# First four weight units opened together in four banks and taken by input block, in five pieces

## The chip, the cores and the metric

One core of one Trainium2 chip runs the program. The metric is the device time of one execution in microseconds (us). Engines: PE multiplies matrices, DVE and ACT work on vectors, POOL sets constants, SP issues transfers; ACT issues some too.

## What is computed

Two transformer blocks over 256 tokens of width 1024, in float32. The change touches only the beginning: the first norm and the first input projection.

```python
def first_block(x, mem, norm_mix, w_in, ...):
    h = h + hybrid_mixer(rmsnorm(h, norm_mix[i]), w_in[i], ...)
...
    proj = n @ w_in
    z, xBC, dt_raw, q, k, v, r, a1, g_ssd, g_gla = jnp.split(proj, idx, axis=-1)
```

## The kernel before

**Units.** All large weights come as a stream of 366 weight units `w[u]`, each 128 x 1024 floats (512 KB): 128 output columns, and 1024 inputs as eight blocks of 128 (`KB` = 8). A ring of four slots holds them (`raw`, `RING` = 4). Unit u goes into slot u % 4.

**Exact products.** Each operand is split into a high part and a low part of lower precision. ACT makes the high part of a unit (`split_hi`, L1163, `whi`), DVE the low part as a difference (`split_lo`, L1670, `wlo`). The input is split likewise, one block at a time: `xh` by ACT (L1209), `xl` by DVE (`operand_lo`, L1677). A unit is then three products for each of its eight blocks, high x high, high x low, low x high: 24 products of 256 columns, added up in one bank of `acc` (four banks, unit u in bank u % 4). DVE empties a bank by multiplying it with `rstd` (an eviction, L1828), the reciprocal root of the mean square that the norm needs. So units can be multiplied before the norm is known, but a bank can't be emptied before.

**Order.** Each engine has its own program, and semaphores tie them. SP issues units 0, the two halves of x, unit 1, the small weights `wsmall`, units 2 and 3; after that it issues a unit when `split_lo` has freed its slot (L380). ACT issues the parameters `par`.

- PE: 14 warm-up products (L713), unit 0 block by block as `xl` comes (L476 to L478), unit 1 (L717, L718, L721), `small_products` (L596 to L598), `stream_stats` (the mean squares, L559 and L563), then the loop over m = 2, 3, ...: `unit`, and after m = 3 the gates (L609).
- ACT: unit 0's high part, eight `xh`, unit 1's, eight squares of x (L1167) with the small weights between them, units 2 and 3, then `rms` (the root, L1181, L1183).
- DVE: unit 0's low part, eight `xl`, unit 1's low part, sums of the squares (L1763 to L1773), units 2 and 3, `inverse_rms` (L1710 to L1715: `rstd`, and `rstdh`, half of it), then the loop: eviction, taps of the convolution (L1795), low part of unit m + 4. At m = 0 it also reads the small products.

ACT's loop makes the high part of unit m + 4, then the first tap of the evicted bank; at m = 1 it loads a table and computes a softplus.

Of the kernel before, what the change touches and what calls it, by code (L numbers as in the profile page):

```python
# [23 lines left out]
P = 128  # L24
F32 = mybir.dt.float32
# [4 lines left out]
ALU = mybir.AluOpType  # L30
# [97 lines left out]
NPAR = _c  # L128
CHUNK_AT = {38: (0, 2), 40: (1, 3), 43: (4, 5)}
# [18 lines left out]
def blocks_kernel(nc, w, wsmall, wa2, par, xT, memT, metaT, out):  # L148
    with ExitStack() as ctx:
# [160 lines left out]
        def hidden(T):  # L310
# [12 lines left out]
        par_in, x_in, x2_in, meta_in, ws_in, wa_in, mem_in = [sem(n) for n in  # L323
            ("par_in", "x_in", "x2_in", "meta_in", "ws_in", "wa_in", "mem_in")]
# [41 lines left out]
        def _(sp_):  # L366
            sp_.dma_start(raw[:, 0, :], w[0, :, :]).then_inc(landed[0], 16)
            sp_.dma_start(hT[:, 0:4, META:T2], xT[:, 0:4, :]).then_inc(x_in, 16)
            sp_.dma_start(hT[:, 4:8, META:T2], xT[:, 4:8, :]).then_inc(x2_in, 16)
            sp_.dma_start(raw[:, 1, :], w[1, :, :]).then_inc(landed[1], 16)  # L370
            sp_.dma_start(wsr, wsmall).then_inc(ws_in, 16)
            for j in range(2, RING):
                sp_.dma_start(raw[:, j, :], w[j, :, :]).then_inc(landed[j], 16)
# [99 lines left out]
        def _(pe):  # L473
# [236 lines left out]

            pe.wait_ge(consts, 2)
            for n in range(14):
                nc.tensor.matmul(mix[:, 2, 0:P], mean1024[:, :], mean1024[:, :], start=True, stop=True)  # L713
            unit("xbc", 0, 0, xh1, xl1, T1, ready=(xl_ready, 0))
            pe.wait_ge(hi_ready, 2)
            for k in range(KB):
                nc.tensor.matmul(acc[:, 1, 0:T1], whi[:, 1, k, :], xh1[:, k, 0:T1], start=k == 0, stop=False)  # L717
                nc.tensor.matmul(acc[:, 1, 0:T1], whi[:, 1, k, :], xl1[:, k, 0:T1], start=False, stop=False)  # L718
            pe.wait_ge(lo_ready, 2)
            for k in range(KB):  # L720
                last = nc.tensor.matmul(acc[:, 1, 0:T1], wlo[:, 1, k, :], xh1[:, k, 0:T1], start=False, stop=k == KB - 1)  # L721
            last.then_inc(unit_done, 1)
            small_products()
            pe.wait_ge(consts, 15)
            stream_stats("mix", T1, tiles1)
            m = 0
            for phase, count in (("xbc", 12), ("q", 4), ("k", 4), ("v", 8), ("z", 8), ("r", 8), ("gs", 8), ("gg", 8)):
                for n in range(count):
# [3 lines left out]
                    elif m > 1:  # L732
                        unit(phase, n, n % 4, xh1, xl1, T1)
                    if m == 3:
                        gla_gates(0)
                        gla_gates(1)
# [419 lines left out]
        def _(act):  # L1156
            def split_hi(base, units=0):

                j = base % 4
                act.wait_ge(landed[j], units * 4 + 16 * (base // 4 + 1))  # L1160
                if base >= RING:
                    act.wait_ge(unit_done, units + (base - 3))
# [37 lines left out]
            act.dma_start(pr[:, :], par).then_inc(par_in, 16)  # L1200
            load_tables(3)
            split_hi(0)
            act.wait_ge(par_in, 16)
            for b in range(KB):
                if b == 4:
                    act.wait_ge(x2_in, 16)
                elif b == 0:
                    act.wait_ge(x_in, 16)
                act.activation(xh1[:, b, 0:T1], hT[:, b, META:T2], ACT.Copy, scale=g("mix", b)).then_inc(xh_ready, 1)  # L1209
            split_hi(1)  # L1210
            act.dma_start(wa[32:48, :], wa2).then_inc(wa_in, 16)
            for b in range(4):
                square(b, T1)
            act.wait_ge(ws_in, 16)
            act.activation(wsh[:, :, :].rearrange("p k c -> p (k c)"), wsr, ACT.Copy).then_inc(ws_ready, 1)
            for b in range(4, KB):
                square(b, T1)
            split_hi(2)
            split_hi(3)
# [445 lines left out]
        def _(dve):  # L1665
# [90 lines left out]
            dve.wait_ge(par_in, 16)  # L1756
            dve.tensor_scalar(halfc, pr[:, PC["convw"]:PC["convw"] + 60], 0.5, None, ALU.mult).then_inc(conv_step, 1)
            split_lo(0)
            for b in range(KB):
                operand_lo("mix", b, T1, b)  # L1760
            split_lo(1)
# [755 lines left out]
```

## Time and profile before

| | us |
|---|---|
| median of 3 runs | 1177.02 |
| lowest, highest | 1176.98, 1177.11 |
| span of the profiled execution | 1175.6 |
| PE busy in it | 1160.9 (99%) |
| DVE busy | 839.4 (71%) |
| ACT busy | 678.9 (58%) |

Times in the profile count from the start of the span. PE is busy nearly all the time; what it does at the beginning, and what it waits for there, is read from the list of waits and the timeline.

### The profile page before, as it was taken

To read this page: it belongs to the slowest core of one execution; us is meant where nothing else is said; L and a number is where in the kernel's file an instruction comes from. 1 tells how busy PE (TensorE), PEld (TensorE's weight loads), DVE (VectorE), ACT (ScalarE), POOL (GpSimd) and SP (SyncE) were. 2 spreads that over 40 slices of the span, in tenths; PEclk is the share of its full clock that TensorE was granted. 3 is DMA by queue.
4 is the path that set the end of the run, shared out by engine and by line. 5 is a ranking of instruction groups with operands and counts; after the bars stand their busy time and mean duration, and the time that the engine had idled before them with its cause. 6 is when DMAs were issued, how large, how long until landed. Compare 5 with 4: busy or idle time off the path is not lost.

```text
span 1175.6 us, 25261 instructions
## 1 busy us (share of the span) xinstructions
PE 1160.9 (99%) x9580; PEld 1140.0 (97%) x9580; DVE 839.4 (71%) x1249; ACT 678.9 (58%) x1029; POOL 46.6 (4%) x68
## 2 busy tenths in 40 slices
PE   8999999999999999999999999999999999999997
PEld 8999899999999999999999999999999999999997
DVE  7998767987856877776667748666545898776453
ACT  6755547656535666655556647656444777665442
POOL 2002311400000000000000000000000000000000
PEclk9999999999999999999999999999999999999998
DMA  6655434566553565656553426555565545666561
GB/s 226 190 174 175 128 107 143 183 225 187 164 159 126 164 201 190 191 185 189 180 152 113 123 73 209 176 171 190 190 180 170 160 144 165 212 182 193 182 194 54
DMA packets 56775, 197.51 MB, mean 168 GB/s; under 512 B 7153, under 2 KB 9457, under 8 KB 56577
## 3 DMA queue, kind: packets, MB, share of 16 engines
q1 hardware_dynamic: 54480, 193.68, 53.8%
q10 hardware_dynamic: 2224, 2.84, 0.8%
q8 instruction: 51, 0.84, 0.3%
q14 instruction: 20, 0.16, 0.0%
HBM read 195.45 MB, written 1.05 MB: 167 GB/s over the span
## 4 chain that ended last, share of the span: by engine, by line
PE 85%; DVE 9%; ACT 4%; issue 2%; DMA 0%; DVEq 0%; ACTq 0%
PE acc L482 14%; PE acc L483 14%; PE acc L488 14%; PE acc L476 11%; PE acc L478 11%; PE acc L477 11%; DVE wlo L1670 3%; ACT whi L1163 1%; PE acc L541 1%; PE acc L542 1%; PE acc L545 1%; PE mix L822 1%; PE mix L803 1%; DVE softp L2166 1%; DVE sp L2156 1%
## 5 line engine op out<-in xcount | busy, mean ns | idle before, releaser
L1670 DVE TENSOR_TENSOR wlo<-raw,whi 128x1024 fp32r<-128x1024 f32 x366 | 448.7, 1229 | 180.0 <-ACT whi L1163 179.8
L1163 ACT ACTIVATE whi<-raw 128x1024 fp32r<-128x1024 f32 x366 | 385.2, 1057 | 317.7 <-PE acc L488 158.5
L482 PE MATMUL acc<-xh,whi 128*128 128x256 f32 (+1 forms) x1448 | 358.2, 285 | 0.0
L483 PE MATMUL acc<-xl,whi 128*128 128x256 f32 (+1 forms) x1448 | 353.7, 282 | 0.0
L482 PEld LDWEIGHTS acc<-xh,whi 128*128 128x128 f32 x1448 | 271.8, 188 | 2.9 <-issue 2.3
L483 PEld LDWEIGHTS acc<-xl,whi 128*128 128x128 f32 x1448 | 272.7, 188 | 0.3
L488 PE MATMUL acc<-xh,wlo 128*128 128x256 f32 (+1 forms) x1448 | 202.2, 282 | 0.0
L478 PE MATMUL acc<-hh,wlo 128*128 128x256 f32 (+1 forms) x688 | 194.4, 283 | 0.0
L476 PE MATMUL acc<-hh,whi 128*128 128x256 f32 (+1 forms) x688 | 194.3, 282 | 0.0
L477 PE MATMUL acc<-hl,whi 128*128 128x256 f32 (+1 forms) x688 | 194.1, 282 | 0.0
L488 PEld LDWEIGHTS acc<-xh,wlo 128*128 128x128 f32 x1448 | 185.2, 188 | 0.0
L477 PEld LDWEIGHTS acc<-hl,whi 128*128 128x128 f32 x688 | 129.4, 188 | 0.0
L478 PEld LDWEIGHTS acc<-hh,wlo 128*128 128x128 f32 x688 | 129.3, 188 | 0.0
L476 PEld LDWEIGHTS acc<-hh,whi 128*128 128x128 f32 x688 | 129.3, 188 | 0.0
L476 PE MATMUL acc<-xh,whi 128*128 128x256 f32 (+1 forms) x272 | 77.3, 284 | 3.3 <-DVE xl L1677 3.3
L478 PE MATMUL acc<-xh,wlo 128*128 128x256 f32 (+1 forms) x272 | 76.6, 282 | 0.0
L477 PE MATMUL acc<-xl,whi 128*128 128x256 f32 (+1 forms) x272 | 76.6, 281 | 0.0
L476 PEld LDWEIGHTS acc<-xh,whi 128*128 128x128 f32 x272 | 51.1, 188 | 3.9 <-DVE wlo L1670 2.4
L482 PE MATMUL acc<-yh,whi 128*128 128x256 f32 (+1 forms) x224 | 54.3, 281 | 0.0
L483 PE MATMUL acc<-yl,whi 128*128 128x256 f32 (+1 forms) x224 | 54.3, 280 | 0.0
L477 PEld LDWEIGHTS acc<-xl,whi 128*128 128x128 f32 x272 | 51.2, 188 | 0.0
L478 PEld LDWEIGHTS acc<-xh,wlo 128*128 128x128 f32 x272 | 51.1, 188 | 0.0
(397 smaller groups left out, 1572.1 us busy)
## 6 DMA issues: line engine op xcount, KB each, us to landing
raw<-w SPq DMA_DIRECT2D x366, 512.0 KB, 3.7
hT<-xT SPq DMA_DIRECT2D x2, 512.0 KB, 6.3
mem<-memT ACTq DMA_DIRECT2D x1, 1024.0 KB, 7.3
rgw<-w ACTq DMA_DIRECT2D x2, 512.0 KB, 4.9
out<-hT SPq DMA_DIRECT2D x4, 128.0 KB, 2.5
out<-hT ACTq DMA_DIRECT2D x4, 128.0 KB, 2.8
xdt<-wsmall SPq DMA_DIRECT2D x1, 192.0 KB, 7.0
pr<-par ACTq DMA_DIRECT2D x1, 114.0 KB, 4.4
```

Source lines behind the costliest of these rows:

```text
L476: nc.tensor.matmul(dst, whi[:, slot, n, :], rh, start=first, stop=False)
L477: nc.tensor.matmul(dst, whi[:, slot, n, :], rl, start=False, stop=False)
L478: return nc.tensor.matmul(dst, wlo[:, slot, n, :], rh, start=False, stop=last)
L482: nc.tensor.matmul(dst, whi[:, slot, n, :], rh, start=first, stop=False)
L483: nc.tensor.matmul(dst, whi[:, slot, n, :], rl, start=False, stop=False)
L488: ins = nc.tensor.matmul(dst, wlo[:, slot, k, :], rh(k), start=False, stop=last and k == KB - 1)
L541: nc.tensor.matmul(dst, ah[:, k, at:at + n], whi[:, s:s + 2, k, :], start=k == 0, stop=False)
L542: nc.tensor.matmul(dst, al[:, k, at:at + n], whi[:, s:s + 2, k, :], start=False, stop=False)
L545: last = nc.tensor.matmul(dst, ah[:, k, at:at + n], wlo[:, s:s + 2, k, :], start=False, stop=k == KB - 1)
L803: last = nc.tensor.matmul(mix[:, h % 2, 256 * t:256 * t + 256], xqT[:, 2 * h + i, P * t:P * t + P], xkT[:, 2 * h + i, :], start=i == 0, st ...
L1163: act.activation(whi[:, j, :, :].rearrange("p k c -> p (k c)"), raw[:, j, :], ACT.Copy)\
L1670: dve.tensor_tensor(wlo[:, j, :, :].rearrange("p k c -> p (k c)"), raw[:, j, :], whi[:, j, :, :].rearrange("p k c -> p (k c)").bitcast(F32 ...
```

## The change

Units 0 to 3 are multiplied together, block by block, each into its own bank. Their weights and x come in five pieces by input block (`PIECES`): one block, one block, and three times two. A piece of weights is one transfer that takes the same blocks of all four units: 512 B (pieces 0, 1) or 1 KB (pieces 2 to 4) out of each 4 KB row. The first two pieces of x are issued by ACT, ahead of its table load, with only the eight columns of `par` that `xh` needs; the rest of `par` goes last on SP's queue. ACT splits a piece of x, then a piece of weights for all four units in one instruction; DVE follows with the low parts. PE takes a block in three groups of four products (high x high, high x low, low x high over the four units), and the last piece unit by unit. Then come the statistics, then the small products, then unit 4. The warm-up has 11 products. The slots of the ring are all freed by the last low part. The gates come after unit 4 and the small products are read by DVE at m = 1.

```diff
+PIECES = ((0, 1), (1, 2), (2, 4), (4, 6), (6, 8))
...
-            sp_.dma_start(raw[:, 0, :], w[0, :, :]).then_inc(landed[0], 16)
-            sp_.dma_start(hT[:, 0:4, META:T2], xT[:, 0:4, :]).then_inc(x_in, 16)
-            sp_.dma_start(hT[:, 4:8, META:T2], xT[:, 4:8, :]).then_inc(x2_in, 16)
-            sp_.dma_start(raw[:, 1, :], w[1, :, :]).then_inc(landed[1], 16)
+            for n, (a, b) in enumerate(PIECES):
+
+                if n >= 2:
+                    sp_.dma_start(hT[:, a:b, META:T2], xT[:, a:b, :]).then_inc(x_in[n], 16)
+                sp_.dma_start(raw[:, :, P * a:P * b], w[0:RING, :, P * a:P * b].rearrange("j p c -> p j c"))\
+                    .then_inc(w_in[n], 16)
             sp_.dma_start(wsr, wsmall).then_inc(ws_in, 16)
-            for j in range(2, RING):
-                sp_.dma_start(raw[:, j, :], w[j, :, :]).then_inc(landed[j], 16)
+            sp_.dma_start(pr[:, KB:NPAR], par[:, KB:NPAR]).then_inc(par_in, 16)
...
+            def open_block(k, n):
+
+
+                pe.wait_ge(xh_ready, k + 1)
+                pe.wait_ge(open_hi, n + 1)
+                for j in range(RING):
+                    nc.tensor.matmul(acc[:, j, 0:T1], whi[:, j, k, :], xh1[:, k, 0:T1], start=k == 0, stop=False)
+                pe.wait_ge(xl_ready, k + 1)
+                for j in range(RING):
+                    nc.tensor.matmul(acc[:, j, 0:T1], whi[:, j, k, :], xl1[:, k, 0:T1], start=False, stop=False)
+                pe.wait_ge(open_lo, n + 1)
+                for j in range(RING):
+                    nc.tensor.matmul(acc[:, j, 0:T1], wlo[:, j, k, :], xh1[:, k, 0:T1], start=False, stop=False)
+
             pe.wait_ge(consts, 2)
-            for n in range(14):
+            for n in range(11):
                 nc.tensor.matmul(mix[:, 2, 0:P], mean1024[:, :], mean1024[:, :], start=True, stop=True)
-            unit("xbc", 0, 0, xh1, xl1, T1, ready=(xl_ready, 0))
-            pe.wait_ge(hi_ready, 2)
-            for k in range(KB):
-                nc.tensor.matmul(acc[:, 1, 0:T1], whi[:, 1, k, :], xh1[:, k, 0:T1], start=k == 0, stop=False)
-                nc.tensor.matmul(acc[:, 1, 0:T1], whi[:, 1, k, :], xl1[:, k, 0:T1], start=False, stop=False)
-            pe.wait_ge(lo_ready, 2)
-            for k in range(KB):
-                last = nc.tensor.matmul(acc[:, 1, 0:T1], wlo[:, 1, k, :], xh1[:, k, 0:T1], start=False, stop=k == KB - 1)
-            last.then_inc(unit_done, 1)
-            small_products()
+            for n, (a, b) in enumerate(PIECES[:-1]):
+                for k in range(a, b):
+                    open_block(k, n)
+            pe.wait_ge(hi_ready, RING)
+            pe.wait_ge(xl_ready, KB)
+            for j in range(RING):
+                for k in range(*PIECES[-1]):
+                    high_products(acc[:, j, 0:T1], j, k, xh1[:, k, 0:T1], xl1[:, k, 0:T1], False)
+                if j == 0:
+                    pe.wait_ge(lo_ready, RING)
+                low_products(acc[:, j, 0:T1], j, range(*PIECES[-1]), lambda k: xh1[:, k, 0:T1], True)\
+                    .then_inc(unit_done, 1)
             pe.wait_ge(consts, 15)
             stream_stats("mix", T1, tiles1)
+            small_products()
             m = 0
             for phase, count in (("xbc", 12), ("q", 4), ("k", 4), ("v", 8), ("z", 8), ("r", 8), ("gs", 8), ("gg", 8)):
                 for n in range(count):
                     if phase == "v":
                         if n % 2:
                             token_pair(phase, n - 1, xh1, xl1, tiles1)
-                    elif m > 1:
+                    elif m >= RING:
...
-                    if m == 3:
+                    if m == 4:
...
-            act.dma_start(pr[:, :], par).then_inc(par_in, 16)
+            act.dma_start(pr[:, 0:KB], par[:, 0:KB]).then_inc(mixw_in, 16)
+            for n in range(2):
+                act.dma_start(hT[:, n, META:T2], xT[:, n, :]).then_inc(x_in[n], 16)
             load_tables(3)
-            split_hi(0)
-            act.wait_ge(par_in, 16)
-            for b in range(KB):
-                if b == 4:
-                    act.wait_ge(x2_in, 16)
-                elif b == 0:
-                    act.wait_ge(x_in, 16)
-                act.activation(xh1[:, b, 0:T1], hT[:, b, META:T2], ACT.Copy, scale=g("mix", b)).then_inc(xh_ready, 1)
-            split_hi(1)
+            act.wait_ge(mixw_in, 16)
+            for n, (a, b) in enumerate(PIECES):
+                act.wait_ge(x_in[n], 16)
+                for k in range(a, b):
+                    act.activation(xh1[:, k, 0:T1], hT[:, k, META:T2], ACT.Copy, scale=g("mix", k)).then_inc(xh_ready, 1)
+                act.wait_ge(w_in[n], 16)
+                act.activation(whi[:, :, a:b, :].rearrange("p j k c -> p j (k c)"), raw[:, :, P * a:P * b], ACT.Copy)\
+                    .then_inc(*((hi_ready, RING) if b == KB else (open_hi, 1)))
+                if n:
+                    for k in range(a if n > 1 else 0, b):
+                        square(k, T1)
             act.dma_start(wa[32:48, :], wa2).then_inc(wa_in, 16)
-            for b in range(4):
-                square(b, T1)
             act.wait_ge(ws_in, 16)
             act.activation(wsh[:, :, :].rearrange("p k c -> p (k c)"), wsr, ACT.Copy).then_inc(ws_ready, 1)
-            for b in range(4, KB):
-                square(b, T1)
-            split_hi(2)
-            split_hi(3)
+            act.wait_ge(par_in, 16)
             rms("mix", T1, (P, P))
...
-            dve.wait_ge(par_in, 16)
-            dve.tensor_scalar(halfc, pr[:, PC["convw"]:PC["convw"] + 60], 0.5, None, ALU.mult).then_inc(conv_step, 1)
-            split_lo(0)
-            for b in range(KB):
-                operand_lo("mix", b, T1, b)
-            split_lo(1)
-            dve.wait_ge(sq_ready, 4)
-            dve.tensor_tensor(sq[:, 2:4, 0:T1], sq[:, 0:2, 0:T1], sq[:, 2:4, 0:T1], ALU.add).then_inc(sum_ready, 1)
-            dve.wait_ge(ws_ready, 1)
-            dve.tensor_tensor(wsl[:, :, :].rearrange("p k c -> p (k c)"), wsr,
-                              wsh[:, :, :].rearrange("p k c -> p (k c)").bitcast(F32), ALU.subtract)\
-                .then_inc(wsl_ready, 1)
+            dve.wait_ge(mixw_in, 16)
+            for n, (a, b) in enumerate(PIECES):
+                for k in range(a, b):
+                    operand_lo("mix", k, T1, k)
+                dve.wait_ge(*((hi_ready, RING) if b == KB else (open_hi, n + 1)))
+                dve.tensor_tensor(wlo[:, :, a:b, :].rearrange("p j k c -> p j (k c)"), raw[:, :, P * a:P * b],
+                                  whi[:, :, a:b, :].rearrange("p j k c -> p j (k c)").bitcast(F32), ALU.subtract)\
+                    .then_inc(*((lo_ready, RING) if b == KB else (open_lo, 1)))
+                if b == 4:
+                    dve.wait_ge(sq_ready, 4)
+                    dve.tensor_tensor(sq[:, 2:4, 0:T1], sq[:, 0:2, 0:T1], sq[:, 2:4, 0:T1], ALU.add).then_inc(sum_ready, 1)
             dve.wait_ge(sq_ready, KB)
             dve.tensor_tensor(sq[:, 6:8, 0:T1], sq[:, 4:6, 0:T1], sq[:, 6:8, 0:T1], ALU.add).then_inc(sum_ready, 1)
             dve.wait_ge(sum_ready, 2)
             dve.tensor_tensor(sq[:, 6:8, 0:T1], sq[:, 2:4, 0:T1], sq[:, 6:8, 0:T1], ALU.add).then_inc(sum_ready, 1)
             dve.wait_ge(sum_ready, 3)
             dve.tensor_tensor(sq[:, 7, 0:T1], sq[:, 6, 0:T1], sq[:, 7, 0:T1], ALU.add).then_inc(sum_ready, 1)
-            split_lo(2)
-            split_lo(3)
+            dve.wait_ge(ws_ready, 1)
+            dve.tensor_tensor(wsl[:, :, :].rearrange("p k c -> p (k c)"), wsr,
+                              wsh[:, :, :].rearrange("p k c -> p (k c)").bitcast(F32), ALU.subtract)\
+                .then_inc(wsl_ready, 1)
+            dve.wait_ge(par_in, 16)
+            dve.tensor_scalar(halfc, pr[:, PC["convw"]:PC["convw"] + 60], 0.5, None, ALU.mult).then_inc(conv_step, 1)
             inverse_rms("mix", T1, (P, P), halved=True)
...
-                    if m == 0:
+                    if m == 1:
```

## Rows read from the trace of the kernel before

**Rows 1.** The page, busy time of the engines.
```profile
PE 1160.9 (99%) x9580; PEld 1140.0 (97%) x9580; DVE 839.4 (71%) x1249; ACT 678.9 (58%) x1029; POOL 46.6 (4%) x68
```
**Rows 2.** Waits of PE, 0 to 60 us: total, times, longest.
```profile
PE acc L476 <- DVE xl L1677: 2.2, 1, 2.2
```
**Rows 3.** Timeline of PE: start us, us, engine line op tile, count.
```profile
1.20 4.85 PE L713 MATMUL mix<-mean 128*128 128x128 f32 x28 [1.20 <-POOL mean L404]
8.30 0.36 PE L476 MATMUL acc<-xh,whi 128*128 128x256 f32 x1 [2.24 <-DVE xl L1677]
...
11.47 0.34 PE L717 MATMUL acc<-xh,whi 128*128 128x256 f32 x1
...
14.34 0.28 PE L596 MATMUL mix<-xh,wsh 128*48 128x256 f32 x1
...
17.14 0.60 PE L559 MATMUL mix<-sq,mean 128*128 128x256 f32 x2
...
17.94 0.36 PE L482 MATMUL acc<-xh,whi 128*128 128x256 f32 x1
...
23.71 1.99 PE L609 MATMUL mix<-xdt,bcn 16*128 16x256 f32 x8
25.63 0.38 PE L482 MATMUL acc<-xh,whi 128*128 128x256 f32 x1
```
**Rows 4.** Timelines of ACT and of DVE, the same columns.
```profile
5.08 1.06 ACT L1163 ACTIVATE whi<-raw 128x1024 fp32r<-128x1024 f32 x1 [2.53 <-DMA raw<-w]
7.12 2.90 ACT L1209 ACTIVATE xh<-hT,pr 128x256 fp32r<-128x256 f32 x7 [0.99 <-DMA hT<-xT]
...
11.28 1.32 ACT L1167 ACTIVATE sq<-hT 128x256 f32<-128x256 f32 x4
...
14.15 1.99 ACT L1163 ACTIVATE whi<-raw 128x1024 fp32r<-128x1024 f32 x2
...
7.66 3.29 DVE L1677 SCALAR_TENSOR_TENSOR xl<-hT,pr,xh 128x256 fp32r<-128x256 f32 x8
11.41 1.23 DVE L1670 TENSOR_TENSOR wlo<-raw,whi 128x1024 fp32r<-128x1024 f32 x1 [0.46 <-ACT whi L1163]
...
14.28 0.69 DVE L1769 TENSOR_TENSOR sq<-sq 128x512 f32<-128x512 f32 x1 [0.48 <-ACT sq L1167]
...
15.73 0.43 DVE L1773 TENSOR_TENSOR sq<-sq 128x256 f32<-128x256 f32 x1
...
20.57 0.29 DVE L1715 TENSOR_SCALAR rstdh<-rstd 128x256 f32<-128x256 f32 x1
...
21.62 0.41 DVE L1828 TENSOR_TENSOR convin<-acc,rstd 128x256 f32<-128x256 f32 x1
```
**Rows 5.** Transfers: count, KB, us from issue to landing; issues 0.81, 1.26, 1.73, 2.27, all.
```profile
raw<-w SPq DMA_DIRECT2D x1, 512.0 KB, 4.2
hT<-xT SPq DMA_DIRECT2D x1, 512.0 KB, 5.8
hT<-xT SPq DMA_DIRECT2D x1, 512.0 KB, 6.8
raw<-w SPq DMA_DIRECT2D x1, 512.0 KB, 7.6
raw<-w SPq DMA_DIRECT2D x366, 512.0 KB, 3.7
```
**Rows 6.** Windows: us, busy PE, PEld, DVE, ACT, POOL; clock, DMA share, GB/s.
```profile
2.00:3.00 1.00, 1.00 (x7) 1.00 (x6) 0.00 (x0) 0.55 (x1) 1.00 (x3) 1.00 0.99 144
...
7.00:8.00 1.00, 0.00 (x0) 0.00 (x0) 1.00 (x2) 0.88 (x3) 1.00 (x2) 1.00 1.12 423
```
**Rows 7.** Packets moved in 5.0 to 5.5, 6.5 to 7.0, 10.0 to 10.5 us.
```profile
DMA packets 133, 0.14 MB, mean 272 GB/s; under 512 B 0, under 2 KB 133, under 8 KB 133
DMA packets 192, 0.19 MB, mean 389 GB/s; under 512 B 5, under 2 KB 191, under 8 KB 192
DMA packets 56, 0.20 MB, mean 401 GB/s; under 512 B 7, under 2 KB 7, under 8 KB 56
```

More of the change, by code:

```diff
@@ L322, in blocks_kernel @@
         consts = sem("consts")
-        par_in, x_in, x2_in, meta_in, ws_in, wa_in, mem_in = [sem(n) for n in
-            ("par_in", "x_in", "x2_in", "meta_in", "ws_in", "wa_in", "mem_in")]
+        par_in, mixw_in, meta_in, ws_in, wa_in, mem_in = [sem(n) for n in
+            ("par_in", "mixw_in", "meta_in", "ws_in", "wa_in", "mem_in")]
+        x_in = [sem(f"x_in{n}") for n in range(len(PIECES))]
+        w_in = [sem(f"w_in{n}") for n in range(len(PIECES))]
+        open_hi, open_lo = sem("open_hi"), sem("open_lo")
         xh_ready, xl_ready, sq_ready = sem("xh_ready"), sem("xl_ready"), sem("sq_ready")
@@ L1159, in split_hi @@
                 j = base % 4
-                act.wait_ge(landed[j], units * 4 + 16 * (base // 4 + 1))
-                if base >= RING:
-                    act.wait_ge(unit_done, units + (base - 3))
+                act.wait_ge(landed[j], units * 4 + 16 * (base // 4))
+                act.wait_ge(unit_done, units + (base - 3))
                 act.activation(whi[:, j, :, :].rearrange("p k c -> p (k c)"), raw[:, j, :], ACT.Copy)\
```

## The prediction

> **What bounds the kernel now.** I read the page's busy table first: TensorE (PE) is busy 1160.9 of 1175.6 us [rows 1]. So the kernel is a PE stream that starts late, and only two things can shorten it: an earlier start, or fewer holes. The list of PE's waits up to 60 us names one wait for data, 2.2 us ahead of the first real product [rows 2]. The PE timeline shows the rest [rows 3]: warm-up from 1.20 to 6.05, a hole, first product at 8.30, then unit 0 (to 11.47), unit 1 (to 14.34), the 24 small products (14.34 to 17.14, so 2.80 us, 0.1167 us each), the statistics (to 17.94), units 2 and 3 (to 23.71, 2.88 us each) and the gates. From 8.30 on there is no hole; unit 0 takes 3.17 instead of 2.80 us, because xl is made one block each 0.41 us [rows 4].
>
> Why 8.30: weight unit 0 lands at 5.06 (issued 0.81, 4.2 us to landing; ACT starts its high part at 5.08), the first half of x at 7.06 (issued 1.26, 5.8 us) [rows 4, 5]. So the hole is a wait for x, which stands behind a whole unit of weights in the queue.
>
> **Yardstick.** At 23.71 PE has done units 0 to 3, the small products and the statistics. The changed kernel does the same work and goes on with unit 4 (the gates, 1.92 us, come one unit later, which is neutral). If its opening (the four units) ends at T, the gain is 23.71 less the time at which unit 4 can begin. All later stages are the same PE stream and shift with it.
>
> **From T to unit 4.** Statistics now come first, then the small products: 0.80 + 2.80, so PE is free at T + 3.6. But unit 4 needs bank 0 emptied, and that needs rstd. Before, the statistics began at 17.14, DVE's halved rstd (the step after rstd) ended at 20.86, and an eviction takes 0.41 [rows 3, 4]. So from the start of the statistics bank 0 is free after 3.72 + 0.41 + about 0.1 for the semaphore, 4.25 us, and PE waits some 0.65 us ahead of unit 4: a new hole. It was covered before, since units 2 and 3 went into empty banks while rstd was made. Hence **gain = 23.71 - 4.25 - T = 19.46 - T.**
>
> **What the opening needs.** 96 products at 0.1167 are 11.2 us. Let H(n) be the time at which ACT has finished the high part of piece n. The first eight products of a block take 0.93 us, then its low part must be there. DVE's low part of 1024 columns takes 1.23 [rows 4], so after a piece that PE stood waiting for, it waits about 0.35 us more. Pieces 2, 3 and 4 hold two blocks each (2.8 us of PE). So T is the largest of:
> - S + 11.2, S being the first product. By the rate below piece 0 lands near 4.7; its 512 columns take ACT 0.6 (a little over half of the 1.06 for 1024 [rows 4]). So S is 5.3 and this is 16.5;
> - H(2) + 0.35 + 8.4 + 0.1 for the semaphores, H(2) + 8.9;
> - H(3) + 6.1;
> - H(4) + 3.65 (here PE has only 4 products to do before it waits for the low part, so that wait is 0.85).
>
> The early start is therefore worth nothing by itself: if piece 2 comes late, PE does blocks 0 and 1 (2.8 us) and stands.
>
> **When the pieces come.** ACT's own work between piece 1's landing and H(2) is 0.6 for piece 1, two squares (1.32 for 4, so 0.66), two xh (2.90 for 7, so 0.82) and 1.0 for piece 2 (1.99 for two units), 3.1 us in all [rows 4]. So H(2) is the later of (piece 1 landed + 3.1) and (piece 2 landed + 1.05). The bytes: 0.39 MB a piece (w 0.262, x 0.131) for 0 and 1, and 0.787 for 2, 3 and 4; in sum 0.79 MB by piece 1, 1.57 by piece 2, 3.15 by piece 4. Little flows before 3.0 us (144 GB/s in the third microsecond); I count 0.15 MB [rows 6]. A transfer is reported landed some 0.9 us after the queue has moved all bytes up to its end: adding up the seven microseconds from 1 to 8 (the second and the last stand in rows 6), 0.641 MB (unit 0 and par) were through at 4.3 and reported at 5.06, and 1.69 MB (with all of x) at 7.4 and reported at 8.5 [rows 5, 6].
>
> The unknown is the rate r for this mixture. Weights now come in packets of 512 B (pieces 0, 1) and 1 KB. No row has 512 B. With 4 KB rows the queue moves 401 GB/s; pure 1 KB packets (x) go at 272 GB/s in one half microsecond and at 389 in another [rows 7]. The bounds are 200 GB/s (512 B packets a little quicker each than the slow 1 KB ones) and 400 (no loss). I take 320, a little under the middle of the two 1 KB rows, since five sixths of the bytes are in 1 KB packets.
>
> By r = 320: piece 1 lands at 3.0 + 0.64/0.32 + 0.9 = 5.9, piece 2 at 8.35, piece 3 at 10.8, piece 4 at 13.25. H(2) is the later of 9.0 and 9.4. T is the largest of 16.5, 9.4 + 8.9 = 18.3, 11.85 + 6.1 = 17.95 and 14.3 + 3.65 = 17.95. So T = 18.3 and the gain is **1.16 us**. By r = 400, H(2) is 8.6 (ACT's chain now binds), T = 17.5, gain 1.96. By r = 272, T = 19.6 (piece 4 binds), a loss of 0.15.
>
> A rule speaks against the change here. The Trainium skill, DMA: Bandwidth & Descriptors, "Why small descriptors are slow (HBM only)", says that each packet costs about three bus cycles beside its 32-byte beats; from that I estimate 512 B packets at 0.86 and 1 KB packets at 0.94 of the rate of 4 KB ones. By that rule r would be near 370 and the gain about 1.7 us; the 389 row agrees with it, the 272 row doesn't.
>
> **What costs nothing, and its cover.** Three warm-up products fewer (14 took 4.85 us, so 1.04 less [rows 3]) end the warm-up at 5.0, before S. The granted clock stayed at 1.00, the 2.4 GHz level, through the old hole of 2.2 us [rows 6], so a hole of this size costs only itself. The sums of the squares on DVE (14.28 to 16.16 before [rows 4]) follow the last low part and end near H(4) + 3.2, before T. wsmall and the rest of par now go last on SP's queue, behind 3.1 MB; they land near 14 and are wanted after T. Weight units 4 to 7 are issued only after the last low part (H(4) + 1.3, near 15.6) and all at once; a unit lands 3.7 us after its issue [rows 5], so unit 4 is there near 19.5 and its high part, behind ACT's root, near 21, against PE's 22.5. That cover is 1.5 us. Behind the eviction, DVE's work per unit (eviction 0.41, low part 1.23, taps) and ACT's table load and softplus are the same, but PE now stands 3.6 us closer to them. Adding their rows up, the high part of unit 6 comes about 1 us before PE wants it and the tightest eviction (unit 5's) 0.5 us. So I put no wait there.
>
> **Rivals.**
> - *Pieces come as quickly as 4 KB rows, and ACT's chain is shorter than I add.* T is 16.5 to 17.4, the time 1174.1 to 1175.0. For it: the 389 row. Against: ACT's 3.1 us cannot start before piece 1 is there, whose 0.79 MB is more than the 0.641 that landed at 5.06. Chance 0.12.
> - *Arrival becomes the bound (slower).* If runs of 512 B and 1 KB picked out of four units at once move at 200 to 250 GB/s, H(4) decides: at 250, piece 4 lands at 15.9, T = 20.6, 1178.2; at 200, T = 23.6, 1181.2. The break-even is r = 275; a loss of 0.2% is passed at r = 227. For it: the 272 row, and that every read now takes an eighth or a quarter of a 4 KB row. Against: 389 GB/s a microsecond later. Chance 0.13. The skill's DMA: Bandwidth & Descriptors, "Rules for kernel authors", asks to coalesce small transfers because mostly overhead is paid; here unit 1, queued behind x, was reported 1.4 us after it [rows 5], so no fixed cost is paid in series.
> - *The closeness costs.* DVE's low parts or ACT's table load come after PE wants them, in units 5 to 9, for 1 to 2 us in sum: 1176.9 to 1177.9. For it: margins of 0.5 to 1 us only. Against: DVE needs about 2.4 us a unit there, PE 2.8. Chance 0.10.
> - *Forecast*, r between 272 and 400: 1175.0 to 1177.2. Chance 0.65.
>
> **The numbers.** The profiled execution spans 1175.6 us; the median is 1177.02, so 1.4 us lie outside it and don't change. 1177.02 - 1.16 = 1175.9. Two tenths of a per cent, about what a measurement of this kernel can tell from no change, are 2.35 us, so faster means under 1174.67: most of the first rival, 0.09. Slower means over 1179.37: the second rival's slow end, 0.08. The range 1174.7 to 1178.4 leaves about 0.1 out on either side.
>
> **What would show it.** First product at 5 to 5.5; PE standing near 8 for about a microsecond, released by the high part of piece 2; opening over near 18.3; 0.65 us of idle time ahead of unit 4, released by the eviction; no hole afterwards. Wrong if the wait sits at piece 3 or 4 (r below 272), if there is none at all, or if holes show between units 5 and 9.

## The result: slower by a quarter of a per cent

| | before | after |
|---|---|---|
| median, us | 1177.44 (10 runs) | 1180.69 (10 runs) |
| span of the profiled execution, us | 1175.6 | 1178.2 |
| ratio after / before | | 1.0024 [1.0015, 1.0033] |

A gain of 1.16 us was forecast and a range of 1174.7 to 1178.4; the changed kernel is about 3 us slower and lies outside it. The ten runs of before that stand beside it have a median 0.4 us above that of the first three. One of the ten runs of the changed kernel took 4042.79 us, for a reason that nothing here shows, and the ratio is that of the other nine. Between the two profiled executions the change lost 2.6 us, and the traces show where.

PE first: the busy times, and all waits of PE up to 200 us (total, times, longest), in the profile of after. The lines are those of the changed kernel, 5 to 23 higher than before.

```profile
PE 1162.8 (99%) x9574; PEld 1140.5 (97%) x9574; DVE 839.3 (71%) x1250; ACT 679.1 (58%) x1030; POOL 46.2 (4%) x68
```
```profile
PE mix L732 <- POOL mean L409: 1.2, 1, 1.2
PE acc L722 <- ACT whi L1231: 1.1, 2, 0.9
PE mix L651 <- DVE bcn L1845: 1.0, 2, 0.5
PE acc L487 <- DVE convin L1851: 0.6, 1, 0.6
PE mix L636 <- DVE xdt L1942: 0.6, 1, 0.6
PE acc L546 <- ACT vt L1326: 0.4, 1, 0.4
PE mix L628 <- DVE xc L1916: 0.2, 1, 0.2
```

From 60 to 200 us the list of before has one line:

```profile
PE mix L646 <- DVE bcn L1822: 1.0, 2, 0.5
```

The 2.2 us wait for xl [rows 2] is gone, and the wait for bcn is as long as it was. The waits for whi and for convin, 1.7 us together, are of the kind that the forecast has. The last three are not: they are new, and they lie at 82 to 93 us, still within the first projection, at m = 23 to 25 of the loop, where the values' units are multiplied. PE's timeline in after, at the places that matter (start, time in the group, line, tile, count, idle time before):

```profile
8.45 0.71 PE L722 MATMUL acc<-xh,whi 128*128 128x256 f32 x4 [0.16 <-ACT whi L1231]
...
10.99 0.71 PE L722 MATMUL acc<-xh,whi 128*128 128x256 f32 x4 [0.91 <-ACT whi L1231]
...
19.81 0.59 PE L564 MATMUL mix<-sq,mean 128*128 128x256 f32 x2
24.19 0.36 PE L487 MATMUL acc<-xh,whi 128*128 128x256 f32 x1 [0.61 <-DVE convin L1851]
...
29.11 0.38 PE L487 MATMUL acc<-xh,whi 128*128 128x256 f32 x1
...
83.54 0.67 PE L628 MATMUL mix<-xc 128*128 128x256 f32 x2 [0.15 <-DVE xc L1916]
...
86.35 0.36 PE L546 MATMUL acc<-whi,xh 128*128 128x256 f32 x1 [0.40 <-ACT vt L1326]
...
93.30 0.66 PE L636 MATMUL mix<-ident,xc 128*128 128x128 f32 x4 [0.59 <-DVE xdt L1942]
93.72 0.42 PE L651 MATMUL mix<-cs,sel 128*128 128x384 f32 x1
```

The same work in the timeline of before:

```profile
28.54 0.28 PE L482 MATMUL acc<-xh,whi 128*128 128x256 f32 x1
...
82.45 0.59 PE L623 MATMUL mix<-xc 128*128 128x256 f32 x2
...
84.55 0.36 PE L541 MATMUL acc<-whi,xh 128*128 128x256 f32 x1
...
91.11 0.42 PE L646 MATMUL mix<-cs,sel 128*128 128x384 f32 x1
```

The opening is over (T) at 19.81, and unit 4 starts at 24.19 where before had reached that point at 23.71 [rows 3]. So PE leaves the opening only about half a microsecond late (0.57 us at unit 5, 28.54 against 29.11). Three holes later it is 1.09 us late at 83.54, 1.80 at 86.35 and **2.61 at 93.72**. (The starts are what counts here: the idle times listed add up to less, since the ends of products are modelled.) That is the whole loss; from there to the end it stays at 2.4 to 2.6.

DVE tells why. Its idle times between 20 and 90 us in before:

```profile
27.86 1.22 DVE L1670 TENSOR_TENSOR wlo<-raw,whi 128x1024 fp32r<-128x1024 f32 x1 [1.32 <-ACT whi L1163]
42.39 1.22 DVE L1670 TENSOR_TENSOR wlo<-raw,whi 128x1024 fp32r<-128x1024 f32 x1 [0.31 <-ACT whi L1163]
54.91 1.23 DVE L1670 TENSOR_TENSOR wlo<-raw,whi 128x1024 fp32r<-128x1024 f32 x1 [0.61 <-ACT whi L1163]
84.93 1.23 DVE L1670 TENSOR_TENSOR wlo<-raw,whi 128x1024 fp32r<-128x1024 f32 x1 [1.96 <-ACT whi L1163]
```

and in after, with the three instructions that follow the statistics ahead of them:

```profile
21.52 1.74 DVE L1731 RECIPROCAL rstd<-rt 128x256 f32<-128x256 f32 x1
23.29 0.29 DVE L1735 TENSOR_SCALAR rstdh<-rstd 128x256 f32<-128x256 f32 x1
23.62 0.42 DVE L1851 TENSOR_TENSOR convin<-acc,rstd 128x256 f32<-128x256 f32 x1
...
30.55 1.23 DVE L1690 TENSOR_TENSOR wlo<-raw,whi 128x1024 fp32r<-128x1024 f32 x1 [1.29 <-ACT whi L1184]
45.08 1.23 DVE L1690 TENSOR_TENSOR wlo<-raw,whi 128x1024 fp32r<-128x1024 f32 x1 [0.32 <-ACT whi L1184]
57.61 1.23 DVE L1690 TENSOR_TENSOR wlo<-raw,whi 128x1024 fp32r<-128x1024 f32 x1 [0.61 <-ACT whi L1184]
87.62 1.23 DVE L1690 TENSOR_TENSOR wlo<-raw,whi 128x1024 fp32r<-128x1024 f32 x1 [1.96 <-ACT whi L1184]
```

The same four waits have the same length, each 2.69 or 2.70 us later. From rstdh (20.57 in [rows 4], 23.29 here, 2.72 later) to 87.6 us DVE's program is moved as one rigid piece and makes nothing up: it is busy nearly all the time, and its few waits, for ACT's next high part, are as long as before, so ACT moves with it. The busy time of the engines in stretches of 10 us shows it in before already (PE, PEld, DVE, ACT, POOL, then clock, DMA share, GB/s):

```profile
30.00:40.00 10.00, 10.00 (x88) 9.87 (x87) 9.89 (x21) 5.06 (x8) 0.00 (x0) 1.00 0.53 160
...
60.00:70.00 10.00, 10.00 (x88) 10.00 (x87) 10.00 (x20) 5.90 (x9) 0.00 (x0) 1.00 0.69 197
70.00:80.00 10.00, 10.00 (x87) 10.00 (x86) 9.87 (x15) 3.29 (x4) 0.00 (x0) 1.00 0.57 168
```

DVE has 71% of the whole span [rows 1] but 94 to 100% of each 10 us from 30 to 80.

### The profile page after: what moved, and what is told of

Its sections match the earlier page's. It is cut to its first block, busy times and chain, and to the rows that moved or that the text cites. A ratio compares the mean times of both kernels' runs of the same rounds, so it can differ in the third digit from the quotient of the medians.

```text
span 1178.2 us, 25266 instructions
## 1 busy us (share of the span) xinstructions
PE 1162.8 (99%) x9574; PEld 1140.5 (97%) x9574; DVE 839.3 (71%) x1250; ACT 679.1 (58%) x1030; POOL 46.2 (4%) x68
## 4 chain that ended last, share of the span: by engine, by line
PE 86%; DVE 8%; ACT 4%; issue 1%; DMA 1%; SPq 0%; DVEq 0%; ACTq 0%
PE acc L487 15%; PE acc L488 15%; PE acc L493 15%; PE acc L481 11%; PE acc L483 10%; PE acc L482 10%; DVE wlo L1690 3%; ACT whi L1184 1%; PE acc L547 1%; PE acc L550 1%; PE acc L546 1%; DMA raw<-w 1%; PE mix L844 1%; PE mix L825 1%; DVE softp L2189 1%
## 5 line engine op out<-in xcount | busy, mean ns | idle before, releaser
L1690 DVE TENSOR_TENSOR wlo<-raw,whi 128x1024 fp32r<-128x1024 f32 x362 | 443.7, 1228 | 177.5 <-ACT whi L1184 177.3
L1184 ACT ACTIVATE whi<-raw 128x1024 fp32r<-128x1024 f32 x362 | 381.1, 1057 | 308.2 <-PE acc L493 153.7
L487 PE MATMUL acc<-xh,whi 128*128 128x256 f32 (+1 forms) x1440 | 356.4, 285 | 0.6 <-DVE convin L1851 0.6
L493 PEld LDWEIGHTS acc<-xh,wlo 128*128 128x128 f32 x1440 | 184.2, 188 | 0.0
L481 PE MATMUL acc<-xh,whi 128*128 128x256 f32 (+1 forms) x264 | 74.7, 283 | 1.1 <-DVE xl L1697 1.1
L483 PEld LDWEIGHTS acc<-xh,wlo 128*128 128x128 f32 x264 | 49.6, 188 | 0.0
```

Of the source, the lines that this page charges most:

```text
L481: nc.tensor.matmul(dst, whi[:, slot, n, :], rh, start=first, stop=False)
L483: return nc.tensor.matmul(dst, wlo[:, slot, n, :], rh, start=False, stop=last)
L487: nc.tensor.matmul(dst, whi[:, slot, n, :], rh, start=first, stop=False)
L493: ins = nc.tensor.matmul(dst, wlo[:, slot, k, :], rh(k), start=False, stop=last and k == KB - 1)
L1184: act.activation(whi[:, j, :, :].rearrange("p k c -> p (k c)"), raw[:, j, :], ACT.Copy)\
L1690: dve.tensor_tensor(wlo[:, j, :, :].rearrange("p k c -> p (k c)"), raw[:, j, :], whi[:, j, :, :].rearrange("p k c -> p (k c)").bitcast(F32 ...
```

## Experiments

**Theory D:** from rstd to some 92 us DVE (with ACT behind it) has no slack, and at 82 to 93 us PE has to wait for its results. So the end moves with the start of the statistics, whatever PE does in between. **Theory P**, the one of the prediction: PE's stream sets the end, so it moves with PE's own delay after the opening. Two quantities are compared in each kernel: the start of the statistics less 17.14 [rows 3], and the start of PE's first product of cs and sel less 91.11. PE's own delay is read at its first product of unit 5, against 28.54. Unless a number of executions is given, times in us come from the one profiled execution of each kernel, and ratios from all its runs.

**Statistics late, nothing else.** The kernel before, with the statistics after unit 2:

```diff
-            stream_stats("mix", T1, tiles1)
...
+                    if m == 2:
+                        stream_stats("mix", T1, tiles1)
```

> The kernel before, with only one thing moved: PE does the statistics (0.8 us) after unit 2 instead of ahead of it. PE's work and the transfers at the beginning are those of before. Theory D (DVE's program has no slack from the making of rstd up to about 90 us, so the kernel shifts with the start of the statistics): the statistics move from 17.14 to about 20.0, DVE's first eviction by 2.9 us, and PE stands for it between 80 and 95 us; the time is 2.4 to 2.9 us longer than before. Theory P (PE's stream sets the time from the first product on, as the prediction had it): only a hole of some 0.5 us ahead of the gates, which now wait for the small products to be read; 0.5 to 0.8 us longer than before.

Measured: 1.0027 [1.0015, 1.004]. The statistics start at 19.93 (+2.79), and cs and sel at 93.81 (+2.70): D's number. But it isn't a clean proof: in the profiled execution PE met a hole of 0.47 us and the gates, then the granted clock fell to the 1.2 GHz level for some 3.4 us, so PE itself was 2.06 us late at unit 5.

**DVE with less to do.** One of the taps of the convolution on 16 columns, in after and in before:

```diff
+                n = 16 if tap == 2 else T1
-                ... in0=convin[:, c, tap:tap + T1], ... in1=xc[:, c, :],
+                ... in0=convin[:, c, tap:tap + n], ... in1=xc[:, c, 0:n],
```

> The changed kernel, with DVE's load in the first 60 us cut: tap 2 of the convolution covers 16 of its 256 columns (so most of that tap is left out), about 0.25 us less for each of 12 instructions, 3 us in sum. Theory D: DVE catches up by unit 18, the waits of PE at 82 to 93 us go, and only the 0.6 us that PE itself has lost by unit 5 stays: 1.5 to 2.2 us less than the changed kernel. Rival A (the waits at 82 to 93 us come from ACT, whose exponentials stand ahead of the evictions of the values): no change, within 0.5 us of the changed kernel.

> The control of the run with the light tap: the kernel before with the same cut (tap 2 on 16 of 256 columns, most of it left out). Its PE waits for DVE only 1.0 us in this part of the program. Theory D: 0.3 to 1.1 us less than before, so less than the changed kernel gains from the same cut. If the cut takes 2 us or more off this kernel too, DVE is the bound in both and the cut says nothing on the change.

Measured: after goes to 1.0005 [0.9995, 1.0014], before to 0.9998 [0.9988, 1.0008]. The same relief is worth 0.2% in after and nothing in before. The 0.3 to 1.1 us expected of before didn't come: the 1.0 us that its PE waits for DVE (bcn) lies at 144 and 153 us and stays. PE's waits in the lightened after:

```profile
PE acc L722 <- ACT whi L1231: 3.0, 3, 1.6
PE mix L651 <- DVE bcn L1846: 1.0, 2, 0.5
PE acc L487 <- DVE convin L1852: 0.6, 1, 0.6
```

The three waits at 82 to 93 us are gone. The opening of this execution came late (whi 3.0 instead of 1.1 us, statistics +4.02), PE was 1.92 us behind at unit 5, and cs and sel stand at +2.12: this is theory P's behaviour, once DVE has slack.

**An earlier x.** All x on SP's queue, each piece ahead of its weights:

```diff
+                sp_.dma_start(hT[:, a:b, META:T2], xT[:, a:b, :]).then_inc(x_in[n], 16)
...
-            for n in range(2):
-                act.dma_start(hT[:, n, META:T2], xT[:, n, :]).then_inc(x_in[n], 16)
```

> The changed kernel, with the first two pieces of x issued on SP's queue, each ahead of its weights, in place of ACT's queue, where the second one took 5.4 us to land (7.25) while the weights of the same piece had landed at 5.15. If the two queues' sharing delayed piece 1 and through it ACT: piece 1 complete near 6.0, H(2) near 9.9 instead of 10.85, the opening over near 19.2 instead of 19.81 (piece 4 binds then), and by theory D as by theory P 0.5 to 0.7 us less than the changed kernel. If the queue's rate alone sets piece 2: H(2) within 0.3 us of 10.85 and no change.

Measured: 1.0043 [1.0026, 1.0059]. A miss: the first product came earlier (5.22), the pieces behind it later. The weights of piece 1 were taken up at 7.07 and those of piece 2 at 10.69, so PE waited 0.97 and 2.39 us. Statistics +3.49, cs and sel +3.43, although PE was only 1.36 late at unit 5.

**Statistics a unit earlier.** After, with the statistics ahead of the last products of unit 3:

```diff
+                if j == 2:
+                    pe.wait_ge(consts, 15)
+                    stream_stats("mix", T1, tiles1)
```

> The changed kernel, with the statistics one unit's products earlier: after unit 2's last products instead of unit 3's. Theory D (DVE's chain from rstd on has no slack): they start near 19.1 instead of 19.81 (the sums end at 18.7), everything after 91 us stands where the statistics' shift puts it, about 0.7 us less than the changed kernel. The hole of 0.6 us ahead of unit 4 closes too, because 0.7 us of products now lie behind the statistics, but by theory D that alone is worth nothing: if the hole closes and the shift after 91 us is the statistics' shift less 0.1, D holds; if the time falls by 1.2 us or more, the hole and the chain add up, and D is wrong.

Measured: 1.0021 [1.0011, 1.0031]. The 0.61 us ahead of unit 4 is gone, but the opening again came late in the profiled execution (whi 3.1 us): statistics +3.59, PE 1.47 late at unit 5, cs and sel +3.53. So the 0.7 us of time weren't gained, but the sign of theory D is there: the hole closes, and the later work stands where the statistics put it, less 0.06. An early start of the statistics helps only if the opening allows it.

**DVE's work moved, none left out.** ACT evicts the gates instead of DVE, and the halved rstd is made at m = 26, off the way to the first eviction. This, on the last kernel and on before:

```diff
-            inverse_rms("mix", T1, (P, P), halved=True)
+            inverse_rms("mix", T1, (P, P))
...
+                    if m == 26:
+                        dve.tensor_scalar(rstdh[:, 0:T1], rstd[:, 0:T1], 0.5, None, ALU.mult).then_inc(rstdh_ready, 1)
...
-                            ins = dve.tensor_scalar(gx[:, i, :], mix[:, BANK[f"gate{i // 2}"], ...
+                            ins = act.activation(fl(khk)[:, 256 * i:256 * i + 256], mix[:, BANK[f"gate{i // 2}"], ...
```

> The kernel with the early statistics, and 1.9 us of DVE's work between rstd and 91 us taken off that chain: ACT instead of DVE evicts the four gate tiles (1.64 us), and rstdh (0.3 us) is made at unit 26 instead of right behind rstd. Theory D: DVE's shift of 2.0 us is nearly used up by 80 us, PE's waits at 82 to 93 us mostly go, and what remains is PE's own shift at unit 5, near 0 with the early statistics: 2 to 2.6 us less than the changed kernel, within 0.8 us of the kernel before. Rival A (ACT is what is late at 82 to 93 us): ACT has 2 us more to do, and the time is that of the early statistics or longer.

> The control: the kernel before with the same 1.9 us of DVE's work moved. Theory D: PE waits only 1.0 us for DVE here, so 0 to 0.9 us less than before. If it gains as much as the changed kernel does, the move is worth something by itself and doesn't tell of the change.

Measured: 1.0000 [0.9991, 1.001] and 1.0003 [0.9993, 1.0013]. Again the move is worth 0.2% where the statistics are late, and nothing in before. In the first of the two, statistics +3.40, PE +1.19 at unit 5, cs and sel +1.53, and no wait is left at 82 to 93 us. ACT got the work that DVE lost, so with a late ACT as the cause (rival A) this kernel would have been no faster; that cause is ruled out.

**Fewer, larger pieces.** After with four pieces of two blocks, all x on SP's queue; then the same with early statistics; then with both and DVE's work moved:

```diff
-PIECES = ((0, 1), (1, 2), (2, 4), (4, 6), (6, 8))
+PIECES = ((0, 2), (2, 4), (4, 6), (6, 8))
```

> The changed kernel with four pieces of two blocks (no packets of 512 B for the weights, and fewer transfers) and all of x on SP's queue ahead of its weights. Up to the end of the second piece the same 1.57 MB are moved as by the run with x on SP, in 1536 packets instead of 2048. If the number of packets or transfers sets the arrival, the second piece lands about a microsecond earlier than there (10.7 us); if the bytes set it, at the same time. First product near 7.3 us. The opening ends between 18.9 and 20.6; by theory D the time is that of the kernel before plus the statistics' start less 17.14: 1.7 to 3.5 us longer than before.

> Pieces of two blocks with all of x on SP's queue, and the statistics one unit's products earlier. Theory D gives the shift against the kernel before, from 91 us on, as the start of the statistics less 17.14 and 0.08: they should start near 18.65, so a shift of 1.4 us, 1.0 to 1.8 us longer than before, though PE itself stands no later at unit 5 than before (about 0.5 us earlier). Theory P (PE's stream sets the time) gives 0.5 us less than before.

> The same with the 1.9 us of DVE's work taken off the chain behind rstd (gates evicted by ACT, rstdh made at unit 26). Theory D: DVE's shift of 1.4 us is used up, PE's own shift stays, about 0.5 us less than before; 1.5 to 2.3 us less than the run with the early statistics alone. If the early start were worth its 1 us of PE time once DVE is out of the way, this is the version that shows it.

Measured: 1.0025 [1.0016, 1.0035], 1.0018 [1.0009, 1.0028] and 1.0003 [0.9994, 1.0012]. In the first, PE is no more than 0.09 us late at unit 5, and the kernel still loses 2.2 us of span (statistics +2.22, cs and sel +2.14):

```profile
19.36 0.59 PE L562 MATMUL mix<-sq,mean 128*128 128x256 f32 x2
...
28.63 0.38 PE L485 MATMUL acc<-xh,whi 128*128 128x256 f32 x1
...
93.25 0.42 PE L649 MATMUL mix<-cs,sel 128*128 128x384 f32 x1
```

By theory P this kernel would have been as fast as before. In the second the statistics start at 20.11 and not near the 18.65 expected, because the granted clock fell in its opening (last section). The third has the best opening of all in its profiled execution (statistics at 18.60, PE 0.68 us ahead of before at unit 5, cs and sel at 90.76, so 0.35 ahead) and a span of 1174.9, but its median over eleven runs (1177.74 against 1177.20) doesn't differ from before's. So with larger pieces, and with DVE's delay worked off, the early opening is worth nothing that can be measured here: runs of both kernels spread over more than 2 us, and the trace shows a gain of 0.35.

**What makes the pieces late.** Two single executions of the kernel with four pieces. In one, each transfer of weights of the first two pieces is cut in two by units; in the other, the x of these pieces is issued by ACT:

```diff
-                sp_.dma_start(raw[:, :, P * a:P * b], w[0:RING, :, P * a:P * b].rearrange("j p c -> p j c"))\
+                for j in range(0, RING, 2 if n < 2 else RING):
+                    e = j + (2 if n < 2 else RING)
+                    sp_.dma_start(raw[:, j:e, P * a:P * b], w[j:e, :, P * a:P * b].rearrange("j p c -> p j c"))\
```
```diff
+            for n, (a, b) in enumerate(PIECES[:2]):
+                act.dma_start(hT[:, a:b, META:T2], xT[:, a:b, :]).then_inc(x_in[n], 16)
```

> As e8_two_blocks (pieces of two blocks, all x on SP's queue), but the weights of its first two pieces come in two transfers each, units 0 and 1 and units 2 and 3. The packets are those of e8 (1536 up to the end of the second piece), the transfers are 6 up to there, as in e4_sp_x, instead of 4. In e8 the second piece landed at 9.06 and in e4, with 2048 packets in 6 transfers, at 10.7. If the number and size of the packets set the arrival, the second piece lands at 9.0 to 9.3 here too. If the number of transfers does, it lands at 10 or later, near the 10.7 of e4. One execution is looked at; its span should be e8's 1177.8 in the first case and about 1179.5 in the second.

> As e8_two_blocks, but the x of its first two pieces is issued on ACT's queue, behind the small transfer of the norm's weights, as the changed kernel has it for its first two pieces. In e8 and the two kernels built on it the first piece of x landed at 5.1 to 5.25 and its weights at 6.4 to 6.55; in four executions with the changed kernel's opening the x of the second block, on ACT's queue, landed at 7.3 to 9.2. If a transfer on ACT's queue is late because it shares the engines with the weights that SP issues at the same time, the first x lands after 6.5 here, behind its weights, and the first product is later than e8's 7.64 by a microsecond or more. If ACT's queue is not the cause, the first x lands near 5.2 again, the weights earlier than 6.4, and the first product is at 7.2 to 7.6.

The high part of the weights with which the first 1.57 MB are complete, in ACT's timeline, and what it waited for; first the kernel with four pieces, then with its transfers cut in two, then the one with five pieces all on SP's queue:

```profile
9.11 1.06 ACT L1227 ACTIVATE whi<-raw 128x1024 fp32r<-128x1024 f32 x1 [0.55 <-DMA raw<-w]
```
```profile
9.19 1.06 ACT L1229 ACTIVATE whi<-raw 128x1024 fp32r<-128x1024 f32 x1 [0.55 <-DMA raw<-w]
```
```profile
10.69 1.06 ACT L1227 ACTIVATE whi<-raw 128x1024 fp32r<-128x1024 f32 x1 [0.60 <-DMA raw<-w]
```

Six transfers instead of four cost 0.08 us; six transfers of which four carry the single blocks (1024 packets of 512 B in place of 512 of 1 KB) cost 1.58. So it is the cut into single blocks, the packets of half the size and double the number, and not the count of transfers. These are single executions, but the others agree: in all five executions with single blocks these bytes landed at 9.8 to 10.7 us, in the four with two blocks a piece and x on SP's queue at 8.9 to 9.2. With x on ACT's queue the first split of x in the four-piece kernel moved from 5.19 to this:

```profile
7.94 0.91 ACT L1228 ACTIVATE xh<-hT,pr 128x256 fp32r<-128x256 f32 x2 [4.21 <-DMA hT<-xT]
```

One execution took 1185.82 us against 1177.65 of before. Here x lands with 1 MB of weights that SP issues over the same time; ahead of them on SP's queue it lands first. This kernel is also the sharpest test of D against P: PE is 4.66 us late at unit 5, the statistics 6.76, and cs and sel 6.69.

**All of it together**, in us against before:

| kernel | statistics | PE at unit 5 | cs and sel |
|---|---|---|---|
| after | 2.67 | 0.57 | 2.61 |
| statistics late | 2.79 | 2.06 | 2.70 |
| all x on SP | 3.49 | 1.36 | 3.43 |
| statistics early | 3.59 | 1.47 | 3.53 |
| four pieces | 2.22 | 0.09 | 2.14 |
| four pieces, early | 2.97 | 0.85 | 2.88 |
| four pieces, transfers cut | 2.30 | 0.17 | 2.24 |
| four pieces, x on ACT | 6.76 | 4.66 | 6.69 |
| one tap light | 4.02 | 1.92 | 2.12 |
| early, DVE's work moved | 3.40 | 1.19 | 1.53 |
| four pieces, early, moved | 1.46 | -0.68 | -0.35 |

In the first eight the last column is the first less 0.06 to 0.09, while the middle one ranges from 0.09 to 4.66. In the last three, where DVE has slack, it goes with the middle one and stays 0.2 to 0.34 above it. So theory D is shown up to 92 us, and theory P falls wherever DVE has no slack. Behind that the shift hardly changes: at the last low part of the kernel (1155.94 us in before) it is within 0.22 us of the last column in nine of the eleven. With the transfers cut another 0.7 us is lost on the way, with x on ACT 1.5; these two have one execution each, and the cause stays open.

## Why the prediction was wrong

- **The yardstick failed.** "All later stages are the same PE stream and shift with it" is the wrong step, and "I put no wait there" repeats it. PE had reached 23.71 with a stock of work done; DVE had not. The change puts the statistics behind all four units, and DVE's program hangs on the statistics without slack up to 92 us. The yardstick should have been 17.14, the old start of the statistics, with a loss of T - 17.14, less about 0.06. Even with the T of the forecast, 18.3, that is 1.1 us slower; with the measured 19.81 it is 2.6. The sum of margins that should have caught it took DVE at 2.4 us a unit against PE's 2.8, from eviction, low part and taps. In before DVE is busy 48.84 of the 50 us from 30 to 80, three of whose five windows are shown above, and makes 17 low parts in them: 2.87 us a unit, because the eviction of the gates, the scans and other steps come on top. Of the miss of 3.8 us between the forecast and the profiled executions this step is 2.04 us (0.57 to 2.61).
- **T was 1.5 us off, by the arrival.** The formula held: H(2) was 10.85 (the group at 9.79 below and its 1.06), and H(2) + 8.9 = 19.75 stands against the measured 19.81. H(2) was forecast at 9.4. The rate is one part: the 1.57 MB up to piece 2 were there at about 9.8, so (1.57 - 0.15) / (9.8 - 0.9 - 3.0) = 0.241 MB per us, 241 GB/s instead of 320. The other is that piece 1 came too late as well: its x was there at 7.25 instead of 5.9, and ACT was through with the chain behind it only at 9.72, when the weights of piece 2 landed too (issued at 2.40, 7.4 us to landing). Both set H(2). ACT's timeline of after:

```profile
5.05 0.51 ACT L1229 ACTIVATE xh<-hT,pr 128x256 fp32r<-128x256 f32 x1 [1.36 <-DMA hT<-xT]
...
7.27 0.51 ACT L1229 ACTIVATE xh<-hT,pr 128x256 fp32r<-128x256 f32 x1 [1.20 <-DMA hT<-xT]
...
8.82 0.90 ACT L1229 ACTIVATE xh<-hT,pr 128x256 fp32r<-128x256 f32 x2
9.79 1.06 ACT L1231 ACTIVATE whi<-raw 128x1024 fp32r<-128x1024 f32 x1
```

  The chain was summed at 3.1 us and took 3.58 (7.27 to 10.85): the sum left out the split of piece 1's own x, 0.42 us. The wait was at piece 2 and for the high part, as forecast, but it began at 10.1 us instead of near 8 (0.91 us, after 0.16 at piece 1). The bounds of 200 to 400 GB/s hold the rate, the chosen 320 doesn't.
- **The slow packets were not a matter of size alone.** Packets moved in after from 3.0 to 3.5, 4.5 to 5.0 and 8.0 to 8.5 us:

```profile
DMA packets 342, 0.17 MB, mean 345 GB/s; under 512 B 23, under 2 KB 342, under 8 KB 342
```
```profile
DMA packets 94, 0.09 MB, mean 172 GB/s; under 512 B 4, under 2 KB 94, under 8 KB 94
```
```profile
DMA packets 193, 0.19 MB, mean 383 GB/s; under 512 B 6, under 2 KB 193, under 8 KB 193
```

  The 512 B packets at 3.0 us run at 345 GB/s and the 1 KB ones at 8.0 at 383; the stretch between them is slow, as was the 272 of [rows 7]. Why there is such a stretch stays open. The rule of the Trainium skill, DMA: Bandwidth & Descriptors, "Why small descriptors are slow (HBM only)", from which the prediction estimated a loss of 6 to 14%, is borne out by these fast rows, but the 1.5 us between the five-piece and the cut four-piece kernel are over a quarter of the 5.3 us that the latter's bytes took (from 3.9, which is 3.0 and the 0.9 of a landing, to 9.2): more than it gives.
- **From T to unit 4** was right: 4.38 us against 4.25, and a hole of 0.61 against 0.65, released by the eviction as forecast.
- **The warm-up** didn't end at 5.0: its 11 products took 5.06 us for the 22 instructions (1.21 to 6.2), more than the 28 instructions of before in 4.85. The first product came at 6.22 instead of 5.3. The forecast had scaled the 4.85 us by the count, but PE's speed isn't even there: the first four real products of after start 0.24 us apart, the later ones 0.12, although the clock column shows 1.00 at both. The same 22 instructions took 4.22 us in the kernel with all x on SP, so the end of the warm-up isn't set by their number alone. None of it cost time, since the end of the opening hung on piece 2.
- **The hole of 2.2 us.** From it the prediction read that "a hole of this size costs only itself". The holes of after, 0.91 us at most, did cost only themselves, but it is no rule: in another kernel the granted clock fell behind a hole of 1.88 us (last section).
- **The covers** that the prediction named for par, wsmall and units 4 to 7 held: no row shows a wait for them.
- **The rivals.** "The closeness costs" named the right engines and the right size (1 to 2 us), but looked for the waits in units 5 to 9, where there are none, and got a chance of 0.10. Its margins were added up for PE's next need; the sum should have gone on along DVE's program to where PE first waits for it without any margin. "Arrival becomes the bound" had the right direction for T and the wrong place: with the yardstick used there, T = 19.81 would have cost 0.35 us. The rule on small transfers that it weighs, in the Trainium skill, DMA: Bandwidth & Descriptors, "Rules for kernel authors", speaks of transfers under 64 KB. It doesn't bear on this change, where the smallest transfer of x or weights has 128 KB. The 1.4 us read between the reports of x and unit 1 are 1.3 by their rows, which changes nothing.

## What to carry to other kernels

An engine with 71% of the span can have nearly all of a stretch: before an early step is moved, look at every engine's busy time by stretch, and follow the engine that hangs on the moved step to the place where the bounding engine next waits for it. A step that feeds a full engine is priced by its own start, not by the time at which PE is through with the work around it. A delay that shows in no wait for 60 us need not be absorbed; compare the two timelines at paired instructions of each engine, and the shift names the engine that carries it.

## What the runs showed of the hardware

- **A transfer on ACT's queue gets a share, not a lane.** In four executions with the opening of after, the x of the second block was taken up at 7.27, 8.88, 9.16 and 8.96 us; in four with all x on SP's queue and two blocks a piece, the first x was there at 5.13 to 5.25 and its weights at 6.44 to 6.55. The Trainium skill, DMA: Bandwidth & Descriptors, "Issuing engines are not separate DMA queues", says that transfers of all issuing engines interleave on the same 16 engines; the 7.94 of the kernel with x on ACT agrees. With the five pieces all on SP's queue the x of the second block was taken up at 4.99, and the weights of pieces 1 and 2 behind it at 7.07 and 10.69. Why one opening varies by 1.9 us and the other by 0.1 was not tried.
- **The granted clock after a hole.** The 2.24 us hole of before left it at 1.00 [rows 6], and so did holes of 1.38 to 1.49 us in three kernels with four pieces and one of 2.39 us in the kernel with all x on SP. In the kernel with x on ACT, PE stood for 3.94 us, and it fell; two of its windows, the same columns as above:

```profile
10.00:11.00 1.00, 1.00 (x5) 1.00 (x6) 1.00 (x2) 1.00 (x3) 0.00 (x0) 0.50 1.10 347
...
16.00:17.00 1.00, 1.00 (x10) 1.00 (x10) 0.59 (x3) 1.00 (x2) 0.00 (x0) 1.00 0.00 0
```

  0.50 is the 1.2 GHz level. It lasts from 9.0 to 15.8 us, and PE does 5 to 7 products a microsecond there instead of 10. In the kernel with four pieces and early statistics it fell too, after a hole of only 1.88 us, from 8.7 to 12.1 us:

```profile
8.00:9.00 1.00, 1.00 (x9) 0.81 (x8) 1.00 (x2) 0.49 (x2) 0.00 (x0) 0.86 1.09 383
9.00:10.00 1.00, 1.00 (x5) 1.00 (x6) 0.65 (x3) 1.00 (x2) 0.00 (x0) 0.50 1.12 353
```

  Its first product came at 7.74, that of the kernel with DVE's work moved as well, whose opening is the same, at 7.75; the statistics came at 20.11 and 18.60. So the low level cost 1.5 us, and the length of the hole alone doesn't tell whether the clock falls. In the kernel with late statistics it fell as well, after 0.47 us of waiting and the gates:

```profile
27.00:28.00 1.00, 1.00 (x7) 1.00 (x7) 1.00 (x2) 1.00 (x1) 0.00 (x0) 0.50 0.66 135
```

  These are single executions of each kernel, and what decides stays open.
